# One weight unit of three experts, loaded half by SyncE and half by GpSimd

## What is computed

```python
def swiglu(h, w1, w3, w2):
    return (jax.nn.silu(h @ w1) * (h @ w3)) @ w2

def moe_swiglu(h, w_router, w1, w3, w2):
    xt = h.reshape(-1, d)
    top_val, top_idx = lax.top_k((xt @ w_router).astype(jnp.float32), TOP_K)
    gate = jax.nn.softmax(top_val, axis=-1)
    combine = jnp.sum(jax.nn.one_hot(top_idx, N_EXPERTS) * gate[..., None], axis=1)
    for e in range(N_EXPERTS):
        y = y + combine[:, e:e + 1] * swiglu(xt, w1[e], w3[e], w2[e])
```

## Time and profile before

| | us |
|---|---|
| median of 3 runs | 1172.65 |
| profiled execution, time | 1172.53 |
| profiled execution, span from first to last instruction | 1170.7 |
| PE busy in the span | 1090.9 (93%) |
| DVE, ACT, POOL busy | 326.8, 236.7, 39.4 |
| bytes moved by DMA | 417.88 MB, 357 GB/s in the mean |

### The profile page before, as it was taken

How to read it: one execution, slowest core, us unless ns; L and a number is a source line. 1 busy time by engine, 2 the same in 40 slices (tenths; PEclk the granted TensorE clock), 3 DMA queues, 4 the chain that set the end, 5 groups by cost and what they waited for, 6 DMA issues and landing times.

```text
span 1170.7 us, 25177 instructions
## 1 busy us (share of the span) xinstructions
PE 1090.9 (93%) x11721; PEld 618.6 (53%) x11721; DVE 326.8 (28%) x435; ACT 236.7 (20%) x370; POOL 39.4 (3%) x35
## 2 busy tenths in 40 slices
PE   7999999999999999999989969999996799999776
PEld 6888888889763354364446315333631444454233
DVE  5655555468660030040021003102100220022023
ACT  5586655656620000000000000000000000000002
POOL 3000000011000000000000000000000000000000
PEclk9999999999999999999999989999999899999988
DMA  9986555534279999999999999999999999999993
GB/s 347 387 303 207 180 200 195 180 126 170 106 308 419 423 387 426 425 421 427 424 428 421 426 427 421 426 425 427 421 425 427 423 425 424 427 422 425 427 424 146
DMA packets 58418, 417.88 MB, mean 357 GB/s; under 512 B 5714, under 2 KB 11908, under 8 KB 33988
## 3 DMA queue, kind: packets, MB, share of 16 engines
q1 hardware_dynamic: 56512, 411.21, 86.2%
q0 software_dynamic: 1440, 4.46, 1.0%
q10 hardware_dynamic: 356, 0.54, 0.1%
HBM read 414.09 MB, written 2.10 MB: 356 GB/s over the span
## 4 chain that ended last, share of the span: by engine, by line
PE 64%; DMA 33%; DVE 2%; issue 0%; SPq 0%; ACT 0%; DVEq 0%
DMA weights<-in_moe_w 32%; PE psum L859 22%; PE psum L895 13%; PE psum L765 8%; PE psum L767 8%; PE psum L766 8%; DVE hid_t L1707 1%; DMA raw<-in_pool_w 1%; PE psum L978 1%; DVE sil L1705 1%; PE psum L838 0%; PE psum L773 0%; PE psum L1099 0%; PE psum L874 0%; PE psum L1076 0%
## 5 line engine op out<-in xcount | busy, mean ns | idle before, releaser
L859 PE MATMUL psum<-weights,xg 128*32 128x512 f32 (+1 forms) x5072 | 493.4, 548 | 48.4 <-DMA weights<-in_moe_w 48.3
L859 PEld LDWEIGHTS psum<-weights,xg 128*32 128x32 f32 x5072 | 176.1, 111 | 363.2 <-issue 323.6
L895 PE MATMUL psum<-weights,hid_t 128*32 128x256 f32 x4480 | 247.2, 380 | 13.1 <-DVE hid_t L1707 8.3
L895 PEld LDWEIGHTS psum<-weights,hid_t 128*32 128x32 f32 x4480 | 151.3, 110 | 105.7 <-issue 13.7
L1705 DVE TENSOR_TENSOR sil<-sil,psum 128x1536 f32<-128x1536 f32 (+3 forms) x16 | 21.1, 1321 | 494.5 <-PE psum L859 493.8
L1559 DVE TENSOR_TENSOR low<-raw,high 128x2048 fp32r<-128x2048 f32 x50 | 114.3, 2286 | 95.5 <-ACT high L1263 95.2
L1263 ACT ACTIVATE high<-raw 128x2048 fp32r<-128x2048 f32 x51 | 97.8, 1917 | 54.1 <-PE psum L767 51.0
L1329 ACT ACTIVATE y_hi<-psum 128x768 fp32r<-128x768 f32 (+1 forms) x7 | 5.0, 719 | 491.5 <-PE psum L895 491.5
L765 PE MATMUL psum<-high,a_hi 128*128 128x512 f32 x224 | 87.2, 389 | 0.9 <-DVE a_lo L1596 0.9
L767 PE MATMUL psum<-low,a_hi 128*128 128x512 f32 x224 | 87.2, 389 | 0.0
L766 PE MATMUL psum<-high,a_lo 128*128 128x512 f32 x224 | 87.1, 389 | 0.0
(11 more groups left out here) (244 smaller groups left out, 644.2 us busy)
## 6 DMA issues: line engine op xcount, KB each, us to landing
weights<-in_moe_w SPq DMA_DIRECT2D x128, 1792.0 KB, 35.3
weights<-in_moe_w SPq DMA_DIRECT2D x48, 2048.0 KB, 38.8
raw<-in_ffn_w SPq DMA_DIRECT2D x42, 1024.0 KB, 8.7
weights<-in_moe_w SPq DMA_DIRECT2D x14, 1024.0 KB, 36.4
raw<-in_w_q SPq DMA_DIRECT2D x4, 1024.0 KB, 5.2
raw<-in_w_o SPq DMA_DIRECT2D x4, 1024.0 KB, 5.0
weights<-in_moe_w SPq DMA_DIRECT2D x4, 512.0 KB, 39.3
x_res<-in_x SPq DMA_DIRECT2D x2, 512.0 KB, 5.2
```

What stands on the lines that cost most here:

```text
L859: mm = pe.matmul(UP[c][g * BLK:(g + 1) * BLK, r, :], xg[:, k_, r * BLK:(r + 1) * BLK], w[:, g], start=k_ == 0, stop=k_ == DT - 1)
L895: mm = pe.matmul(Y[g * BLK:(g + 1) * BLK, to, :], hid_t[c][:, r, at_:at_ + BLK], w[:, b, g * GW:(g + 1) * GW], start=i == 0 and b == 0 and ...
```

## The change

In the expert places 2, 4 and 6, unit 8 (the first of w3) is loaded by two engines. SP issues a DMA for the upper 64 rows only. GpSimd, after its gathers for that expert, reads the expert's number, waits for the same count of `unit_used`, and loads the lower 64 rows in eight DMAs of eight rows. Ahead of each it issues a DMA of eight single values (4 bytes in each of eight partitions, from a constant table into an unused column), and behind each pair it waits until that small one has landed. PE waits for both parts. To have semaphores free, the two loads of norm rows now count on one semaphore (`row_in`).

```diff
+UPPER_HALF = slice(P // 2, P)
+SHARED_UNIT = 8
+SHARED_EXPERTS = (2, 4, 6)
+SHARE_ROWS = 8
+SHARES = P // 2 // SHARE_ROWS
...
+        def shared(ps, j, e):
+
+            return not ps.block and e in SHARED_EXPERTS and j == SHARED_UNIT
...
                     sp.wait_ge(unit_used, ps.freed(j, e))
-                    if j < MU - 1:
+                    if shared(ps, j, e):
+                        sp.dma_start(expert_tile(ps, j, e, slice(0, F), UPPER_HALF),
+                                     expert_rows(who, *key, UPPER_HALF)).then_inc(moe_landed[j], 16)
+                    elif j < MU - 1:
...
-            pool.dma_start(row_bc[:], bc(norm_final)).then_inc(gf_in, 16)
+            pool.dma_start(row_bc[:], bc(norm_final)).then_inc(row_in, 16)
...
+            def load_lower_half(ps, e):
+
+                who = pool.value_load(slot_expert[0:1, e:e + 1], min_val=0, max_val=E - 1)
+                pool.wait_ge(unit_used, ps.freed(SHARED_UNIT, e))
+                for n in range(SHARES):
+                    rows = slice(n * SHARE_ROWS, (n + 1) * SHARE_ROWS)
+                    pool.dma_start(over[0:SHARE_ROWS, 1:2], table[0:SHARE_ROWS, 0:1], allow_slow_non_contiguous=True).then_inc(spacer_in, 16)
+                    pool.dma_start(expert_tile(ps, SHARED_UNIT, e, slice(0, F), rows),
+                                   expert_rows(who, *MOE_UNITS[SHARED_UNIT], rows)).then_inc(shares_in, 16)
+                    pool.wait_ge(spacer_in, 16 * (SHARED_EXPERTS.index(e) * SHARES + n + 1))
+
             def expert_pass(ps):
                 for n in range(E):
                     if ps.block or n:
                         gather_rows(ps.n0 + n, ps.blocks(n))
+                    if shared(ps, SHARED_UNIT, n):
+                        load_lower_half(ps, n)
...
                         pe.wait_ge(moe_landed[j], ps.landed(e))
+                    if shared(ps, j, e):
+                        pe.wait_ge(shares_in, 16 * SHARES * (SHARED_EXPERTS.index(e) + 1))
```

More of the change, by code:

```diff
@@ L410, in trunk_program @@
         misc_in, bo_in, rope_in = sem("misc_in"), sem("bo_in"), sem("rope_in")
-        gn_in, gf_in, out_done = sem("gn_in"), sem("gf_in"), sem("out_done")
+        row_in, out_done, shares_in = sem("row_in"), sem("out_done"), sem("shares_in")
         sumsq_ready, var_ready, std_ready = sem("sumsq_ready"), sem("var_ready"), sem("std_ready")
@@ L457, in trunk_program @@
         last_left, last_right, last_scattered = sem("last_left"), sem("last_right"), sem("last_scattered")
+        spacer_in = sem("spacer_in")
         quarter_landed = [moe_landed[MU - 1], moe_landed[MU], sem("third_quarter_landed"), sem("last_quarter_landed")]
@@ L489, in expert_source, with expert_tile, expert_rows @@
             return experts[kind][bass.ds(e, 1), :, i:i + 1, cols].rearrange("o p k f -> p (o k) f")
-        def expert_tile(ps, j, e, cols):
+        def expert_tile(ps, j, e, cols, rows=slice(0, P)):
             start = ps.place(j, e)
-            return weights[:, start + cols.start:start + cols.stop].unsqueeze(1)
+            return weights[rows, start + cols.start:start + cols.stop].unsqueeze(1)
+        def expert_rows(e, kind, i, rows):
+            return experts[kind][bass.ds(e, 1), rows, i:i + 1, :].rearrange("o p k f -> p (o k) f")
+        def shared(ps, j, e):
+            return not ps.block and e in SHARED_EXPERTS and j == SHARED_UNIT
         def moves(t_, group, kk_first):
@@ L727, in _ @@
             pool.wait_ge(bo_added, NT)
-            pool.dma_start(row_bc[:], bc(norm_ffn[1])).then_inc(gn_in, 16)
+            pool.dma_start(row_bc[:], bc(norm_ffn[1])).then_inc(row_in, 16)
             pool.wait_ge(roped, len(ROPE))
@@ L1906, in _ @@
             dve.wait_ge(bo_added, NT)
-            dve.wait_ge(gn_in, 16)
+            dve.wait_ge(row_in, 16)
             for t in range(NT):
@@ L2042, in finish @@
                 dve.tensor_copy(y_last[:, ps.blocks(E - 1) - 1, :], Y[:, NB - 1, :]).then_inc(last_right, 1)
-                dve.wait_ge(gf_in, 16)
+                dve.wait_ge(row_in, 32)
                 for t in range(NT):
```

## The result

The changed kernel takes 1237.99 us (median of 4 runs, 1236.54 to 1239.27) against 1172.91 for the kernel before beside it: a ratio of 1.055, 95% interval 1.0538 to 1.0563. That is 65 us slower. The prediction said 1169.2, and its range ended at 1180.5.

What follows compares the result with a forecast made beforehand. DMA transfers were taken to set the pace. From 1172.53 us, 3.4 came off for the last transfer ending sooner and 0.1 was added for the tiny transfers' completions: 1169.2 us, range 1166.5 to 1180.5.

Steps and rivals of the forecast that it cites:

- What bounds the kernel: From where the experts begin, DMA transfers set the pace at 424 or 425 GB/s; PE has room in every second expert.
- Bytes on SP's queue: Unit 8, three experts: 64 rows instead of 128 on SP save every engine 12 rows of 0.54 us, 6.5 us.
- Bytes on GpSimd's queue: Unit 8, three experts: 192 rows return through GpSimd, 24 per engine of one half at 0.576 us, 13.8 us.
- both ends: GpSimd's rows fall all on the early-finishing eight engines (+7.3 us there, late -6.5) or all on the late-finishing eight.
- The side on which the data fall: Tiny transfers alternating with data keep all 24 data transfers on one engine half; early half guessed, 1169.2 us, chance 0.55.
- the rival in which nothing moves: Eight-row transfers spread over both engine halves alike: +0.4 us, 1172.9 us; chance 0.11.
- the gap between the halves: At the kernel's end, eight engines finish on average 12.8 us after the other eight, growing some 1.8 us per expert.
- the early half: The eight engines finishing first, mean end 1142.7 us; the late half's mean end is 1155.5 us.
- the first rival: GpSimd's data fall on the late engines, which end 7.3 us later: 1179.8 us; chance 0.27 together with doubled early half.
- When the shares land: GpSimd's eight rounds per shared unit, 5 us each, take 43.3 us: 3 us late in expert 2, 1 in expert 4.
- What lateness costs: PE stalls at unit 8, but idle time in following two-block experts hides up to some 14 us, so nothing.
- the rival of the slow rounds: GpSimd rounds of 8 us land the last share 25 us late, 11 unhidden per expert: about 1202 us; chance 0.07.

Runs made afterwards that it cites:

- the strided run: Changed kernel, but the eight rows of each GpSimd transfer lie four partitions apart instead of next to each other: 1197.83 us, 1.0207.
- the runs with turns: Changed kernel without tiny transfers; SP loads odd rows, GpSimd strided even rows alternating between lower and upper 64 partitions: 1186.67 us lower first, 1187.15 us upper first.
- The run with two halves: Against the changed kernel, GpSimd loads nothing; SP loads unit 8 of the three experts as upper and lower 64 rows: 1206.08 us, 1.0281.
- the two mirrors: Changed kernel with GpSimd's eight rows four partitions apart: SP upper, GpSimd lower 64 rows, 1197.83 us; SP lower, GpSimd upper, 1221.31 us.
- the run with rows sixteen apart: Changed kernel, but SP loads the odd rows and GpSimd's eight-row transfers take even rows sixteen partitions apart: 1197.7 us, 1.0211.
- the tiny transfers alone: Changed kernel, but SP loads the whole unit again; GpSimd issues and awaits only the tiny transfers, no data: 1173.57 us, 1.0002.
- the free cuts: Against the changed kernel, GpSimd loads nothing; SP loads unit 8 as odd and even rows, 1173.4 us, or every fourth row in four transfers, 1173.59 us.

## Why the prediction was wrong

**What bounds the kernel: right.** The transfers set the pace, before and after; the GB/s lost in the dips account for 56.4 of the 66.9 us.

**"Bytes on SP's queue" and "Bytes on GpSimd's queue": the step that failed.** It priced a row by its bytes, 0.54 or 0.576 us of one engine, wherever it goes and whoever carries it. For 24 eights that is 13.8 us on eight engines, 6.9 us of all sixteen. Measured, making the rows of the eights strided gave back 40 us (65.1 less 24.5), 1.7 us of all sixteen engines for each eight, on top of the 0.29 for its bytes. SP's 64 rows were to save 6.5 us; two such halves cost 33, and the strided run, whose eights write lower rows only, still lost 24.5 with one such half. The range took its ends from which engines carry the rows, never from what a row does to others, and that is why it missed by 57 us. A warning sign was there: the prediction itself noted that no row shows how 64 rows are spread and that nothing names the engines of an eight-row transfer, and then took the price of the 128-row ones for both ends.

**The side on which the data fall: wrong in its reason.** The forecast let the tiny transfers keep the data on one half, and the Trainium skill's page "DMA: Bandwidth & Descriptors" was cited ("Why a DMA increments its semaphore by 16 and not by 1") for a cursor that goes round. The runs show neither: with nothing between them, eights behave as if they stayed on the same engines (the runs with turns), and one tiny transfer more changes the time by 1.7 us.

**The rule against the change: it deserved more.** The Trainium skill's page "DMA: Bandwidth & Descriptors" says under "Rules for kernel authors" that two transfers to disjoint partition halves aren't worth it. I made it the rival in which nothing moves, at 1172.9. The run with two halves shows that they lose 33 us here.

**The tail.** The last stretches of the changed kernel (columns as in rows 6):

```profile
1202.00:1206.00 4.00, 4.00 (x76) 2.55 (x69) 0.00 (x0) 0.00 (x0) 0.00 (x0) 1.00 0.89 367
1206.00:1210.00 4.00, 4.00 (x80) 2.44 (x76) 0.00 (x0) 0.00 (x0) 0.00 (x0) 1.00 0.49 202
1210.00:1214.00 4.00, 3.04 (x60) 1.59 (x52) 0.00 (x0) 0.00 (x0) 0.00 (x0) 1.00 0.18 72
1214.00:1218.00 4.00, 4.00 (x89) 2.52 (x83) 0.00 (x0) 0.00 (x0) 0.00 (x0) 1.00 0.12 49
1218.00:1222.00 4.00, 4.00 (x92) 2.64 (x88) 3.08 (x4) 0.00 (x0) 0.00 (x0) 1.00 0.15 57
```

The shelf at 0.48 has become one at 0.12 to 0.18: two or three engines at work for 12 us instead of eight. So the gap between the halves closed for most engines, as the forecast's sum had it, and yet the end didn't come sooner. One reading fits the sum: of the eight engines that carry eights, six belong to the early half and two to the late one, and these two end 13.8 - 6.5 = 7.3 us later than before, the first rival's price for two engines. Then the run with turns should lose 12 x 0.7 = 8.4 for its upper eights and 7.3 for its end, 15.7; its span grew by 1184.9 - 1170.7 = 14.2. This was only reckoned; with 23.5 / 24 = 0.98 us for an upper eight, from the two mirrors, the same sum gives 19.1; and the run with rows sixteen apart, whose tail keeps a shelf of a half (0.49 and 0.48 from 1172 to 1180), doesn't fit it. It stays open.

**When the shares land: the round was too short. What lateness costs: right enough.** The first and the last eight of expert 2, issued by GpSimd (start us, us):

```profile
525.66 0.55 POOL L772 DMA_DIRECT2D weights<-in_moe_w  x1
...
578.80 0.52 POOL L772 DMA_DIRECT2D weights<-in_moe_w  x1
```

Seven rounds took 53.1 us, 7.6 each, where the sum took 5. Part of that is the loss itself: with the tiny transfers alone these landed after 5.8 us in the median; in the changed kernel GpSimd waited 137.2 / 21 = 6.5 us for one. So the rounds came near the 8 us of the rival of the slow rounds. But its price did not follow, for PE waited 8.6 us for the shares, and not over 15 in each expert: SP's loads were late as well. In the run with turns PE waited 32.8 us in 3 for the shares, and the transfers went on meanwhile, at a share of 1.00.

**Could the idea work with better shapes?** To take work from the late engines, others must write rows that lie in the late ones' places. The runs priced that: 0.7 us of all sixteen engines for eight such rows, or 0.98 by the mirrors. Moving 96 rows in this way (12 upper eights) costs 8.4 us or more, and a tail of two halves with a gap of 12.8 us can give back 6.4 at most. No kernel here beat the one before; the free cuts end at 1173.3 to 1173.6.

## What to carry to other kernels

Where transfers set the pace, cut a load into pieces of 64 or 32 rows that each reach evenly over all 128 partitions (odd and even rows, or every fourth row), not into blocks of neighbouring partitions: in halves the same bytes cost 0 or 33 us. Eight rows sixteen apart reach evenly too and still cost 24.5 us, so smaller pieces have to be measured. Read GB/s beside the busy share: a share of 0.99 stood beside 280 GB/s, and one of 1.01 beside 425. And where the trace of before doesn't show a shape of transfer, the price of another shape is no bound for it; one run of that transfer beside the real traffic is worth more than a longer sum.

## What the runs showed of the hardware that I had not expected

- Two loads of 64 neighbouring rows on a single queue bring sixteen engines from 425 down to 201 to 221 GB/s at a share of 1.00.
- An eight of strided rows costs 0 or 0.7 us of all engines, depending on whether it writes the lower or the upper 64 partitions (420 to 430 against 378 to 395 GB/s; packets of 535 to 549 against 548 to 1145 ns).
- GpSimd's queue is no slower than SP's for a whole unit of 1,792 KB beside the weights (1173.33 us, ratio 1.0003).
